# Mamba2 heads of a two-block model: weighing, values and scores at other places of TensorE's order, two mask products as one

## The reference

```python
proj = rms_norm_2(h, norm) @ w_in                   # z, xbc (2048 x, 512 B, 512 C), dt
xbc = silu(causal_depthwise_conv(xbc, conv_w, conv_b))
dt = softplus(dt_raw + dt_bias); A = -exp(a_log)
# one chunk of 256 tokens, 32 heads of 64, 4 groups of 8 heads, state 128
cum = cumsum(dt * A)
decay = exp(where(causal, cum[:, None] - cum[None, :], -inf))
cb = einsum("blgn,bsgn->blsg", c, b)                # the scores of a group
y = einsum("blsg,blsge,bsgep->blgep", cb, decay, x * dt) + x * d_skip
y = group_rms_norm(y * silu(z)) * gnorm             # 4 groups
out = y @ w_out
```

## Time and profile before

| | |
|---|---|
| median of 3 runs | 2786.02 us (2781.89 to 2791.76) |
| the profiled execution | 2787.74 us, span 2785.9 us |
| busy share of the span | PE 93%, PEld 86%, POOL 71%, DVE 53%, ACT 48% |
| chain that ended last | PE 71%, DVE 11%, POOL 8%, ACT 4%, issue 3%, DMA 2% |
| mean granted clock of TensorE | 0.966 |

### The profile page before, as it was taken

One profiled execution on the slowest core, in us unless ns is written; L12 is line 12 of the kernel. 1 busy time (PEld: TensorE's weight loads), 2 busy tenths in 40 slices (PEclk: granted clock), 3 DMA queues, 4 the chain that ended last, 5 costly groups with the idle time before them and its releaser, 6 DMA issues.

```text
span 2785.9 us, 49291 instructions
## 1 busy us (share of the span) xinstructions
PE 2595.2 (93%) x19228; PEld 2405.0 (86%) x19228; DVE 1471.8 (53%) x2672; ACT 1349.5 (48%) x2339; POOL 1985.1 (71%) x2181
## 2 busy tenths in 40 slices
PE   6889999998999999999989999888989998899999
PEld 6889889898999888888989987678879997678999
DVE  5776432368727874333467564744454356554541
ACT  4434444555645444445455655541354455455543
POOL 6866557798989866558888985340269996456997
PEclk8999999999999999999999999889999998889999
DMA  6433334454665433335456653120136664223665
GB/s 200 129 87 97 107 106 128 120 151 139 183 173 151 129 91 107 107 107 146 125 147 198 198 160 107 46 76 1 31 114 188 184 175 114 61 83 111 178 187 154
DMA packets 682934, 354.90 MB, mean 127 GB/s; under 512 B 11121, under 2 KB 680913, under 8 KB 682321
## 3 DMA queue, kind: packets, MB, share of 16 engines
q1 hardware_dynamic: 680464, 343.45, 43.1%
q10 hardware_dynamic: 2240, 8.31, 0.8%
HBM read 350.67 MB, written 1.05 MB: 126 GB/s over the span
## 4 chain that ended last, share of the span: by engine, by line
PE 71%; DVE 11%; POOL 8%; ACT 4%; issue 3%; DMA 2%; ACTq 0%; DVEq 0%
PE pb L276 70%; POOL wl L345 8%; ACT pool L299 1%; DVE bx L655 1%; ACT wh L334 1%; DVE xl L784 1%; DVE pool L1078 1%; DMA raw<-in_w_in 1%; DVE bx L3265 1%; PE pb L553 0%; DMA raw<-in_w_ffn_in 0%; DMA raw<-in_ffn_w 0%; DVE pool L952 0%; ACT pool L300 0%; DVE pool L1077 0%
## 5 line engine op out<-in xcount | busy, mean ns | idle before, releaser
L345 POOL TENSOR_TENSOR wl<-raw,wh 128x256 fp32r<-128x256 f32 (+1 forms) x2164 | 1973.9, 947 | 790.9 <-ACT wh L334 790.4
L276 PE MATMUL pb<-xh,wh 128*128 128x272 f32 (+2 forms) x3104 | 947.4, 305 | 27.7 <-POOL wl L345 5.0
L334 ACT ACTIVATE wh<-raw 128x1024 fp32r<-128x1024 f32 (+2 forms) x669 | 690.4, 1034 | 458.5 <-PE pb L276 314.8
L276 PE MATMUL pb<-xl,wh 128*128 128x272 f32 (+2 forms) x3104 | 894.9, 288 | 0.0
L276 PE MATMUL pb<-xh,wl 128*128 128x272 f32 (+2 forms) x3104 | 894.0, 288 | 0.0
L276 PEld LDWEIGHTS pb<-xh,wh 128*128 128x128 f32 x3104 | 596.5, 192 | 55.7 <-issue 18.9
L276 PEld LDWEIGHTS pb<-xl,wh 128*128 128x128 f32 x3104 | 597.4, 192 | 3.3
L276 PEld LDWEIGHTS pb<-xh,wl 128*128 128x128 f32 x3104 | 596.1, 192 | 0.0
L276 PE MATMUL pb<-pool 128*128 128x128 f32 (+15 forms) x2064 | 334.2, 311 | 49.3 <-DVE pool L1078 14.6
L276 PEld LDWEIGHTS pb<-pool 128*128 128x128 f32 (+6 forms) x2064 | 243.4, 179 | 117.7 <-issue 24.2
L276 PE MATMUL pb<-u2h,wh 128*128 128x256 f32 x840 | 242.8, 289 | 4.9 <-DVE u2l L647 4.3
(11 more groups left out here) (374 smaller groups left out, 3841.0 us busy)
## 6 DMA issues: line engine op xcount, KB each, us to landing
raw<-in_w_in SPq DMA_DIRECT2D x208, 512.0 KB, 3.7
raw<-in_ffn_w SPq DMA_DIRECT2D x120, 512.0 KB, 4.0
raw<-in_w_ffn_in SPq DMA_DIRECT2D x88, 512.0 KB, 3.9
raw<-in_w_branch SPq DMA_DIRECT2D x48, 512.0 KB, 3.8
raw<-in_od_w_in SPq DMA_DIRECT2D x41, 512.0 KB, 3.8
raw<-in_w_ffn_out SPq DMA_DIRECT2D x32, 512.0 KB, 4.0
raw<-in_ev_w_in SPq DMA_DIRECT2D x20, 512.0 KB, 3.9
raw<-in_w_out SPq DMA_DIRECT2D x16, 512.0 KB, 3.9
```

The costliest lines, as they stand in the source:

```text
L276: return e.matmul(out, lhsT=l, rhs=r, start=a, stop=z, skip_group_check=True)
L334: E.e.activation(hi, src, ACT.Copy).then_inc(*sig("weight_hi", ("hi", g)))
L345: E.e.tensor_tensor(lo[:, s, :], src[:, s, :], hi[:, s, :].bitcast(F32), SUB).then_inc(*sig("weight_lo", *[("lo", g, i) for i in ks]))
```

## The change

Four things, all in `ssd` and `pe_ssd_row`:
- The scores begin four places later in the generator.
- The weighing of head `t - 1` moves from the first half of step `t` to the second.
- The values of head `t - 2` instead of `t - 1` are multiplied in step `t`. The sum `ssd_y` follows by two steps, (`t` - 5) / 2 in place of (`t` - 3) / 2, and the gates, squares and the norm's start follow it. The loop has two steps more.
- The two mask products of a head become one: its operand `IDR` is read twice (128x2x128), and its result goes to the first and the last third of the row's bank.

```diff
--- before.py
+++ after.py
@@ -3321,7 +3321,10 @@
 
     def ssd(E):
 
+
         while ("x", 23) not in E.done:
+            yield
+        for _ in range(4):
             yield
         for g in range(4):
             E.do("ssd_scores", g)
@@ -3330,18 +3333,16 @@
             yield
         ungated, squares, norms = [], [], iter(())
         t = 0
-        while t < 34 or ungated or squares:
+        while t < 36 or ungated or squares:
             if t < 32:
                 if t % 2 == 0:
                     while ("x", t // 2) not in E.done:
                         yield
                     E.do("ssd_turn", t // 2)
                 E.do("ssd_row", t)
-            if 1 <= t < 33:
-                E.do("ssd_weigh", t - 1)
-            if t % 2 and 3 <= t < 34:
-                E.do("ssd_y", (t - 3) // 2)
-                ungated.append((t - 3) // 2)
+            if t % 2 and 5 <= t < 36:
+                E.do("ssd_y", (t - 5) // 2)
+                ungated.append((t - 5) // 2)
             next(norms, None)
             yield
             if t < 32:
@@ -3349,7 +3350,9 @@
                 if t % 2 == 0:
                     E.do("ssd_turned", t // 2)
             if 1 <= t < 33:
-                E.do("ssd_values", t - 1)
+                E.do("ssd_weigh", t - 1)
+            if 2 <= t < 34:
+                E.do("ssd_values", t - 2)
             for j in squares:
                 E.do("ssd_square", j)
                 if j == 7:
@@ -3415,8 +3418,8 @@
             e.wait_ge(*at("ssd_consts"))
             e.wait_ge(*at("dtt"))
         mm(e, B[:, 0:384], SEL[:, hh:hh + 1].broadcast_to([64, P]), CUR, True, False)
-        mm(e, B[:, 0:P], NGR, IDR, False, False)
-        mm(e, B[:, NS:384], NGR, IDR, False, True).then_inc(*sig("row", ("row", hh)))
+        mm(e, B[:, 0:384].rearrange("p (a b) -> p a b", b=P)[:, 0:3:2, :], NGR, IDR.unsqueeze(1).broadcast_to([P, 2, P]), False,
+           True).then_inc(*sig("row", ("row", hh)))
 
     def a_ssd_exp(E, hh):
         e, B, x = E.e, banks[3 + hh % 2], ER[hh % 4]
```

## The result

The changed kernel takes 2753.77 us (median of 4 runs, 2745.64 to 2759.62) against 2786.25 for the kernel before (median of 4): a ratio of 0.988 with a 95% interval of 0.986 to 0.990. That is 1.2% faster, and 2 us from the 2756 us of the prediction. A second set of four runs of the same kernel, on another occasion, gave 2754.82 us and 0.9885.

What follows compares the result with a forecast made beforehand. TensorE's ordered work, waits and halved clock were taken to bound 2319 to 2500 us. 0.1 - 10.9 - 3.5 - 3.2 - 12.9 = -30.4 us, from the median of 2786.0, gave 2756 us, range 2745 to 2762.

Steps and rivals of the forecast that it cites:

- What bounds the stretch: From 2319 to 2500 us, TensorE's ordered work, 25.8 us of waits and a halved clock losing 18 us set the time.
- Part 1: Head loop: later weighing and values leave 1.0 us of the 11.9 us of weighing waits, -10.9 us.
- three kinds of tile ends: In order: ahead of a step's first half, no wait; ahead of its second, 0 to 0.3 us; without head work, no wait.
- Part 2: Scores four places later: shorter silu wait, new 2.5 us copy wait, +0.1 us in all (bounds -3.5 and +2).
- Part 3: Norm of groups 0 and 1: turns wait 0.7 and 1.0 us in place of 5.2, -3.5 us (bounds 0 and -5.2).
- Part 4: Two mask products of a head in one: 0.10 us gained for each of 32, -3.2 us.
- Part 5: Clock in the changed stretch: most of 42 us at 1.2 GHz goes, -12.9 us (bounds 0 and -18).
- that I can't place: In the changed stretch, 12 us at 1.2 GHz were kept as remaining, out of 42.
- half of it: Rival, chance 0.25: late evacuations are handed on, weighing waits of 5 us stay, -20.7 us, 2765 us.
- The mask product is slow: Rival, chance 0.08: the mask product in two blocks loses 0.29 us a head, +9.3 us, 2768 us.
- the low clock stays: Rival, chance 0.03: more and smaller waits hold TensorE at 1.2 GHz through the whole stretch, +58 us, 2844 us.
- The wait only moves: Rival, chance 0.06: weighing waits return whole one step later and the clock stays, -5 us, 2781 us.

## Why the prediction was right, step by step

The sum was -30.4 us. The stretch shows -36.5 in one profiled execution and -34.5 in the other, the medians -32.5. With the measured value of each part as given below, -10.4 - 1.5 - 3.7 - 2.9 - 17.7 = -36.2. That the median met 2756 to 2 us is in part luck: the traces give 4 to 6 us more than the sum, and a single execution is good to some 10. The steps hold as follows.

- **What bounds the stretch.** That TensorE's own order, its waits and the halved clock set the time holds: the sum above closes with nothing but these, within what the clock's rounding leaves.
- **Part 1, the values a whole step behind the weighing** (-10.9; measured -10.4). The longest wait left was not among the three kinds of tile ends. At the first values no earlier head's values stand beside the chain: only 12 products, a turn, a row and 6 products from 2337.55 to 2340.73, 3.2 us, against the slow chain, here 4.1 us. The nearest of the three is the third, "No wait". The one of 0.27 us (values at 2364.98) is of the second kind, for which 0 to 0.3 was said. The one of 0.22 (2372.38) is of the third: the tile ends at 2368.20, TensorE has work up to 2372.16, and the slow chain ends at 2372.33, 4.1 us behind the tile instead of 3.9. That the room is what counts, and the weighing's own place is not, was not said; the runs with the values half a step earlier and with the weighing early show it.
- **Part 2, the scores** (+0.1; measured -1.5 and +0.5 in the two executions). The +0.5 sets an execution without the low stretch ahead of tile 0 against one with it; against the two edits of the kernel before that are without it too, it is -1.4 and -1.0. The silu's wait fell to 3.63 and 5.15 us, of which the prediction had 3.6 from a wait of 6.5; the copy's new wait is 2.2 instead of 2.5. Its chain stands as told, only with a silu of 0.42 us in place of 0.88, since it starts just ahead of GpSimd's split at 2328.88 (VectorE, then TensorE):

```profile
2327.43 1.52 DVE L3265 SCALAR_TENSOR_TENSOR bx<-pb,vec,bx 128x255 f32<-128x255 f32 x3 [3.36 <-ACT bx L299]
2328.86 0.42 DVE L3304 SCALAR_TENSOR_TENSOR pool<-tb,bx 128x256 f32<-128x256 f32 x1
2329.19 0.42 DVE L3381 COPY pool<-pb 128x256 f32<-128x256 f32 x1
...
2329.66 0.48 PE L276 MATMUL pb<-pool 128*128 128x256 f32 x1 [2.18 <-DVE pool L3381]
```

- **Part 3, the norm** (-3.5 with waits of 0.7 and 1.0; measured -3.7 with 0.15 and 1.31). The lengths on ScalarE, a table load of 1.28 and a logarithm of 0.47, are those of the earlier trace rows. The first wait is shorter because a new one stands ahead of it, which the prediction did not have: the sum product, now right behind a tile's end, waits for VectorE's sum of squares (TensorE, VectorE, ScalarE). With the weighing early that new wait is gone, and the one for `rs` is 0.54.

```profile
2405.63 0.70 PE L276 MATMUL pb<-pool,cst 128*128 128x256 f32 x2 [0.48 <-DVE pool L3502]
...
2408.87 0.41 PE L3396 MATMUL pb<-cst,pool 128*128 128x128 f32 x2 [0.15 <-ACT rs L299]
2417.86 0.41 PE L3396 MATMUL pb<-cst,pool 128*128 128x128 f32 x2 [1.31 <-ACT rs L299]
...
2405.15 0.42 DVE L3502 TENSOR_TENSOR pool<-pool 128x256 f32<-128x256 f32 x1
...
2408.25 0.47 ACT L299 ACTIVATE rs<-pb,sm 128x256 f32<-128x256 f32 x1
```

  The 1.6 us before the sum of norm 2, called unchanged, became 1.1; with the 0.48 the total of these waits is the same. This part depends on the scores: with weighing and values alone the waits for `rs` fell by 1.0 only, and those before the sums of norms rose by 1.1.
- **Part 4, the masks** (-3.2; measured -2.9). The value between the bounds was right: by head it is 0.107, against 0.10. But half of it comes at the projection product behind, and the next product starts 0.22 us behind the mask product's start, outside the 0.12 to 0.2 that were named as the sign. The Trainium skill ("TensorE: Matmul & The Clock Gate", "Wait — 56ns, not 53.3ns?") would have given 0.1 us in all; the measurement decides against it at this place, where the operands change between the products.
- **Part 5, the clock** (-12.9, bounds 0 and -18; measured -17.7 behind the first row). This is the term that was mis-sized. The 12 us at 1.2 GHz kept as "that I can't place" are not there. They were kept because the wait of 2.28 us at 2400.37 brings no low stretch, from which the prediction took it that low stretches and waits are only loosely tied, and because it looked for them at waits of 2 us and more. The trace of the kernel before already says more: behind the first row all six low stretches stand at a wait of 1.77 to 3.43 us, begun in its last part or at most 1.6 us behind it. Two of these waits are under 2 us, and the granted clock is 0.50 from 2429.40 to 2432.80 and from 2450.33 to 2460.00:

```profile
2428.13 0.41 PE L3393 MATMUL pb<-cst,pool 128*128 128x128 f32 x2 [1.77 <-ACT rs L299]
2450.33 1.54 PE L276 MATMUL pb<-pool 128*64 128x256 f32 x4 [1.82 <-DVE pool L3439]
```

  The run with four waits put back shows the tie: four waits of 2.4 to 2.6 us, a low stretch behind each. In the changed kernel no wait behind the scores is over 1.31 us, and there is no low stretch. How large the term is in another execution of the kernel before is open, since there is one trace of it and not every such wait is followed by a low stretch: with the masks alone, five waits of about the same lengths came with some 10 us less of 1.2 GHz.

The rivals: "half of it" had VectorE hand late evacuations on; its wait for ScalarE's first tap is still 20.8 us in all in the changed kernel, so it has room. "The mask product is slow" and "the low clock stays" fell with 0.22 us and 1.00. "The wait only moves" fell for the weighing, and is just what the second pair of score banks did with the copy.

## What to carry to other kernels

Where a product waits for a chain that hangs on a tile's end, count the work that stands on TensorE between the tile's end and that product, at each kind of tile end and at the first one, where the pipeline is not full yet: half a step more of room was worth 23 to 25 us, the place of the weighing itself nothing. Price a wait with the clock that it may take along: four waits of 2.4 to 2.6 us cost 0.6 of their length on top, nine of 0.5 to 2.0 us 0.7 (9.9 us of 13.3). So splitting one long wait into several of 1.5 us is no cure; none followed where the longest was 1.31 us. Take a buffer away from a wait only after asking who uses that buffer next.

## What the runs showed of the hardware

- The traces of the kernel before and of the one with four waits put back have eight waits of 2.27 to 2.60 us for a weighing. The granted clock is 0.91 to 1.00 in the waits themselves; seven are followed by products at 1.2 GHz, at once or some 1.5 us later. One is not, the 2.28 us at 2400.37 in the kernel before, which is followed by:

```profile
2400.40:2403.00 2.60, 2.60 (x15) 1.95 (x16) 1.78 (x3) 0.08 (x1) 1.51 (x2) 1.00 0.01 2
```

  Nor is it alone: of the eight such waits (2.27 to 2.61 us) with the masks alone and with the scores alone three are spared, two of 2.60 and 2.39 us in the one and one of 2.28 in the other, with a clock of 1.00 in the 4.8 to 5.6 us behind each. So 12 of 16 such waits were followed by a low stretch, and why these four were spared stays open. Shorter waits are not safe either: with the values half a step earlier, seven of nine waits of 0.5 to 2.0 us are followed by a low stretch, some 23 us at 1.2 GHz in all.
- A product of 256 columns in two blocks of 128 takes 0.22 us to the next start, 0.06 less than two products of 128, and the product behind it comes 0.05 us sooner (0.221 and 0.119 us against 0.274 and 0.173, means of 30 heads). A projection product of 256 columns among its own kind takes 0.12. Where the operands change, 0.10 us stand between two starts that the columns do not explain.
- The silu of 128x256 on VectorE takes 0.42 us where it starts 0.02 us ahead of GpSimd's split of weights (2328.86) and 0.88 where it starts 0.14 us behind it (2339.79). By the Trainium skill ("SBUF — State Buffer", "SBUF: two separate sides") the two engines lock a shared pair of ports against each other for an instruction; the trace agrees as far as the silu is short where it starts first and long where it starts second; no run here moved the split away to test it.
